# Rotary turn of the retention heads: DMA between partition halves in place of a product with a turning matrix

## The reference, cut to what matters

```python
def head_group_mixer(h, w_in, sb_norm, ret_norm, w_out):
    sb_q, sb_k, sb_v, r_q, r_k, r_v, r_g = jnp.split(h @ w_in, cuts, axis=-1)
    sb_o = stick_breaking(split_heads(sb_q, 8), split_heads(sb_k, 8), split_heads(sb_v, 8))
    ret_o = retention(rotary(split_heads(r_q, 4)), rotary(split_heads(r_k, 4)), split_heads(r_v, 4))
    ...
def rotary(x):          # x of 4 heads, 256 tokens, 128 features
    x1, x2 = xf[..., : d // 2], xf[..., d // 2:]
    return jnp.concatenate([x1 * cos - x2 * sin, x1 * sin + x2 * cos], axis=-1)
```

## Time and profile before

| | |
|---|---|
| median of three runs | 3829.74 us (3826.93 to 3830.98) |
| the profiled execution's own time | 3830.59 us |
| its span | 3828.8 us |
| PE busy | 3766.3 us, 98% |
| DVE busy | 2734.8 us, 71% |
| ACT busy | 1758.6 us, 46% |
| POOL busy | 572.9 us, 15% |
| mean granted TensorE clock | 0.994 |

### The profile page before, as it was taken

How to read it: one execution, slowest core, us unless ns; L and a number is a source line. 1 busy time by engine, 2 the same in 40 slices (tenths; PEclk the granted TensorE clock), 3 DMA queues, 4 the chain that set the end, 5 groups by cost and what they waited for, 6 DMA issues and landing times.

```text
span 3828.8 us, 68647 instructions
## 1 busy us (share of the span) xinstructions
PE 3766.3 (98%) x23022; PEld 3367.8 (88%) x23022; DVE 2734.8 (71%) x4796; ACT 1758.6 (46%) x2739; POOL 572.9 (15%) x244
## 2 busy tenths in 40 slices
PE   8999999999999999999999999999999999999999
PEld 6888888888888889998999999888889999998887
DVE  7867777676863556634578888888534598888887
ACT  3223323223322354456556776333464557774333
POOL 0000000000000000045575000000256680000000
PEclk9999999999999999999999999999999999999999
DMA  6544434454542325563456666777634466666776
GB/s 251 177 159 157 157 131 153 145 180 138 176 138 88 94 67 157 184 200 118 133 187 224 207 209 203 240 241 241 221 127 149 139 229 208 208 211 220 241 241 211
DMA packets 203862, 685.45 MB, mean 179 GB/s; under 512 B 22560, under 2 KB 24864, under 8 KB 194336
## 3 DMA queue, kind: packets, MB, share of 16 engines
q1 hardware_dynamic: 174880, 573.45, 46.4%
q10 hardware_dynamic: 28800, 109.59, 7.9%
HBM read 646.25 MB, written 36.70 MB: 178 GB/s over the span
## 4 chain that ended last, share of the span: by engine, by line
PE 81%; issue 9%; POOL 7%; DVE 2%; ACT 0%; POOLq 0%; DMA 0%; DVEq 0%; ACTq 0%; SPq 0%
PE bank L581 25%; PE bank L583 25%; PE bank L582 25%; POOL low L541 7%; PE bank L1117 2%; PE bank L623 1%; PE bank L676 0%; PE bank L677 0%; PE bank L681 0%; PE bank L784 0%; PE bank L762 0%; DVE h L1615 0%; DVE low L1636 0%; PE bank L651 0%; ACT high L1200 0%
## 5 line engine op out<-in xcount | busy, mean ns | idle before, releaser
L1200 ACT ACTIVATE high<-raw 128x1024 fp32r<-128x1024 f32 x1044 | 1098.8, 1057 | 1221.3 <-PE bank L583 941.5
L581 PE MATMUL bank<-h_lo,high 128*128 128x256 f32 (+1 forms) x4240 | 1321.8, 312 | 1.5 <-POOL low L541 0.9
L583 PE MATMUL bank<-h_hi,low 128*128 128x256 f32 (+1 forms) x4240 | 1318.4, 311 | 0.0
L582 PE MATMUL bank<-h_hi,high 128*128 128x256 f32 (+1 forms) x4240 | 1316.5, 310 | 0.0
L1636 DVE TENSOR_TENSOR low<-raw,high 128x1024 fp32r<-128x1024 f32 x808 | 971.6, 1219 | 82.1 <-ACT high L1200 79.8
L541 POOL TENSOR_TENSOR low<-raw,high 128x1024 fp32r<-128x1024 f32 x240 | 572.7, 2403 | 2584.5 <-ACT high L1200 2551.2
L581 PEld LDWEIGHTS bank<-h_lo,high 128*128 128x128 f32 x4240 | 799.3, 189 | 50.5 <-POOL low L541 1.8
L582 PEld LDWEIGHTS bank<-h_hi,high 128*128 128x128 f32 x4240 | 799.4, 189 | 47.0 <-issue 0.7
L583 PEld LDWEIGHTS bank<-h_hi,low 128*128 128x128 f32 x4240 | 798.7, 188 | 46.5
L581 PE MATMUL bank<-low,weighed_hi 128*128 128x512 f32 x1024 | 400.0, 391 | 8.5 <-DVE weighed_lo L1636 8.5
L583 PE MATMUL bank<-high,weighed_lo 128*128 128x512 f32 x1024 | 399.8, 390 | 0.0
(11 more groups left out here) (298 smaller groups left out, 4554.2 us busy)
## 6 DMA issues: line engine op xcount, KB each, us to landing
raw<-in_experts SPq DMA_DIRECT2D x516, 512.0 KB, 3.4
raw<-in_w SPq DMA_DIRECT2D x176, 512.0 KB, 4.2
late_raw<-in_mod_late ACTq DMA_DIRECT2D x64, 1024.0 KB, 4.8
acts_spill<-acts_out ACTq DMA_DIRECT2D x128, 256.0 KB, 4.0
acts_in<-acts_spill SPq DMA_DIRECT2D x128, 256.0 KB, 3.4
raw<-in_w_in SPq DMA_DIRECT2D x56, 512.0 KB, 3.4
raw<-in_w SPq DMA_DIRECT2D x64, 384.0 KB, 3.1
raw<-in_w SPq DMA_DIRECT2D x64, 320.0 KB, 3.6
```

The source lines that it names most:

```text
L581: pe.matmul(out, a[0], b[1], start=start, stop=False, **more)
L582: pe.matmul(out, a[0], b[0], start=False, stop=False, **more)
L583: return pe.matmul(out, a[1], b[0], start=False, stop=stop, **more)
L1200: act.activation(high[:, slot * UNIT:(slot + 1) * UNIT], raw[:, slot * UNIT:(slot + 1) * UNIT], ACT.Copy)\
```

## The change: what it does

The turning matrix goes, from the constants and from PE. In its place ACT issues DMAs that copy the halves of the partitions of `r_qk` crosswise into `turned`: partitions 64 to 127 to partitions 0 to 63 and the other way round, four tiles (256 KB) in each DMA. Two DMAs for tiles 0 to 3 are issued after the copy of tile 4, two for tiles 4 to 7 after `high_of` of the memory. Each pair has its own semaphore. The sign of the turn moves into the sine table, whose first 64 partitions are negated on the host.

On DVE the rotary work (two products and an addition for each pair of tiles) moves ahead of the wait for z and the maximum; the product with the sine is now made in place in `turned` and no longer reads a bank. The four additions that raise `head_ready` move with it, from behind the masks of the softplus. POOL's wait for `head_ready` and its place stay as they are, and so do ACT's clamp and exponential.

```diff
@@ PE
                 wait("split", KD)
                 T["normed"].next(KD)
-                for c in range(4):
-                    pe.matmul(ps[4 + c][:, :], mix_const("turn_ret"), r_qk[:, 2 * c:2 * c + 2, :], start=True, stop=True)\
-                        .then_inc(S["head_turned"], 1)
                 wait("z_copied", 4)
@@ ACT
-                to_sbuf([r_qk[:, c, :] for c in range(8)])
+                def swap_halves(first):
+
+                    act.wait_ge(S["evacuated"], T["evacuated"].value(first + 14))
+                    for to in (0, HD // 2):
+                        start = HD // 2 - to
+                        act.dma_start(turned[to:to + HD // 2, first * TOK:(first + 4) * TOK],
+                                      r_qk[start:start + HD // 2, first:first + 4, :].rearrange("p c t -> p (c t)"))\
+                            .then_inc(S[f"swapped{first}"], 16)
+
+                to_sbuf([r_qk[:, c, :] for c in range(5)])
+                swap_halves(0)
+                to_sbuf([r_qk[:, c, :] for c in range(5, 8)], first=5)
                 high_of(mem_hi, mem)
+                swap_halves(4)
                 rows_to_sbuf([r_v[:, s, :] for s in range(2)], 4, bank=4)
@@ DVE
+                wait("mix_loaded", 16)
+                for half in range(2):
+                    wait(f"swapped{4 * half}", 32)
+                    for c in (2 * half, 2 * half + 1):
+                        part, other = r_qk[:, 2 * c:2 * c + 2, :], turned[:, c * 512:(c + 1) * 512].rearrange("p (g t) -> p g t", g=2)
+                        for tile, table in ((other, sin_r), (part, cos_r)):
+                            mark(dve.tensor_tensor(tile, tile, table.rearrange("p (g t) -> p g t", g=1)
+                                                   .to_broadcast([P, 2, TOK]), ALU.mult))
+                        settle()
+                        dve.tensor_tensor(part, part, other, ALU.add).then_inc(S["head_ready"], 1)
+
                 wait("z_copied", SBH)
                 mark(dve.tensor_scalar(stick[:, :], z[:, :], 0.0, None, ALU.max))
-
-                wait("mix_loaded", 16)
-                for c in range(4):
-                    wait("head_turned")
-                    mark(dve.tensor_tensor(turned[:, c * 512:(c + 1) * 512].rearrange("p (g t) -> p g t", g=2),
-                                           ps[4 + c][:, :].rearrange("p (g t) -> p g t", g=2),
-                                           sin_r.rearrange("p (g t) -> p g t", g=1).to_broadcast([P, 2, TOK]), ALU.mult))
-                    mark(dve.tensor_tensor(r_qk[:, 2 * c:2 * c + 2, :], r_qk[:, 2 * c:2 * c + 2, :],
-                                           cos_r.rearrange("p (g t) -> p g t", g=1).to_broadcast([P, 2, TOK]), ALU.mult))
                 settle()
...
-                for c in range(4):
-                    dve.tensor_tensor(r_qk[:, 2 * c:2 * c + 2, :], r_qk[:, 2 * c:2 * c + 2, :],
-                                      turned[:, c * 512:(c + 1) * 512].rearrange("p (g t) -> p g t", g=2), ALU.add)\
-                        .then_inc(S["head_ready"], 1)
@@ constants
-            lay([one[n] for n in MIX_CONSTS] + [np.cos(ret), np.sin(ret), decay.reshape(P, -1)]))
+            lay([one[n] for n in MIX_CONSTS] + [np.cos(ret), np.where(i[:, None] < HD // 2, -1, 1) * np.sin(ret), decay.reshape(P, -1)]))
```

More of the change, by code:

```diff
@@ L74 @@
 CONST_COLS = P * len(CONSTS) + 1
-MIX_CONSTS = ["ones64", "tri", "causal", "turn_ret"]
+MIX_CONSTS = ["ones64", "tri", "causal"]
 MIX_COLS = P * len(MIX_CONSTS) + 2 * TOK + RH * SPAN
@@ L89 @@
     "stick_exp": SBH, "broken": 1, "broken_o": 1,
-    "head_turned": 4, "head_ready": 4, "ret_scored": RH, "ret_decayed": RH, "ret_o": 1,
+    "swapped0": 32, "swapped4": 32, "head_ready": 4, "ret_scored": RH, "ret_decayed": RH, "ret_o": 1,
     "head_summed": 3, "head_rooted": 2, "head_inverted": 2, "head_scaled": 2, "mean_ready": 1, "centred": 1, "mixed_ready": 1,
@@ L395, in two_blocks @@
             "head_summed", "head_rooted", "head_inverted", "head_scaled", "head_normed", "head_turned", "head_ready",
+            "swapped0", "swapped4",
             "score_ready", "max_ready", "exp_ready", "prob_ready", "flipped", "flip_copied", "pv_ready", "o_copied",
@@ L1276, in activate_tiles, with to_sbuf @@
                     tile(f, late + n // 4 * 4 + f if is_late else None)
-            def to_sbuf(outs, func=ACT.Copy):
-                for u, out in enumerate(outs):
+            def to_sbuf(outs, func=ACT.Copy, first=0):
+                for u, out in enumerate(outs, first):
                     wait("unit_used")
@@ L2262, in constant_columns @@
     }
[L2263 to L2270, removed]
+    turn = np.zeros((P, P))
+    for c in range(P):
+        if c // 32 % 2 == 0:
+            turn[c + 32, c] = -1
+        else:
+            turn[c - 32, c] = 1
+    one["turn_axial"] = turn
     f = np.float32
```

## The result

| | before | after |
|---|---|---|
| median | 3830.36 us (3826.93 to 3833.64, 6 runs) | 3845.80 us (3844.02 to 3848.12, 6 runs) |
| ratio to before | | 1.0041, 95% interval 1.0031 to 1.0051 |
| span of the profiled run | 3828.8 us | 3846.3 us |
| clock, mean | 0.994 | 0.991 |

The change makes the kernel 15.4 us slower: 3845.8 us, against a forecast of 3842. The two profiled runs differ by more, 17.5 us, because the one after (3848.12 us) is the slowest of its six. First the page of the kernel after: busy time, share of the span, instructions.

A forecast was written before the change was run, and what follows sets the result against it. The prediction took PE as the limit over the whole kernel. Two layers of 5.5 us delay plus 0.8 us clock loss gave 12.6 us on the profiled 3830.6, so 3843.2, or 3842 in medians; range 3824 to 3848.

The forecast's parts named there:

- The gate opens early, the masks take turns with POOL: Before the stick additions: four second-half masks alternate with POOL's parts, 10.7 us instead of 1.4; first stick addition 7.7 us later.
- The taking of turns without the clock: From projections to scores, the delay per layer before any clock loss: +5.5 us, bounds -3.1 to +8.
- The rotary work beside POOL: On DVE before z: rotary instructions alternate with POOL's parts, 2.95 us a turn, done at 1752.0; PE hardly pushed back.
- Turn products off PE: Before the memory keys: 3.13 us of PE products go; keys start 1.5 us earlier once other delays are counted.
- The DMA issues on ACT: Four issues a layer; the last two delay the high parts behind the memory's split by 0.5 us, bounds 0 to 0.8.
- a sign of being wrong: In the r_g units: PE waiting for POOL by more than 1 us each would show the prediction wrong.
- The transfers: 256 KB copies between halves of the on-chip memory: 4 us each, not late even at 10 us.
- The clock: Idle PE before the later stick sums lowers its clock: 0.8 us a layer, out of 0 to 1.7.
- clock falls for longer: Rival, behind PE's wait: clock loss of 1.7 us in full, perhaps twice, a layer; 3843 to 3848, taken as 3846; chance 0.12.
- The sum: Whole kernel, two layers: 2 x (5.5 + 0.8) = 12.6 us slower, 3842 in medians.
- Not slower: Rival: masks and POOL's four parts do not collide, 2.7 us a layer gained, 3824; decided by POOL starting after 1759; chance 0.22.
- DVE gets two instructions to one part: Rival: two DVE instructions pass per POOL part, so masks wait only twice; +2 us a layer, 3834; chance 0.12.

The follow-up runs named there:

- kernel with 24 fillers: The changed kernel with 24 small unused products on PE behind the sum of stick head 3, keeping PE busy in its wait: 3843.15 us, 1.0028.
- late gate: The changed kernel with POOL's gate before unit 32 waiting for all eight softplus masks instead of the rotary sums: 3830.21 us, 1.0002.
- mask in a bank: The changed kernel, its gate still early, with the causal mask copied into free bank 7 and read there by the masks: 3830.38 us, 0.9998.
- moving the issues: The changed kernel with POOL's gate behind the masks and the second pair of DMAs issued ahead of the memory's splits: 3829.65 us, 0.9991.
- the cleared line: The changed kernel, gate early, second DMA pair issued ahead of the memory's splits, mask and cosine and sine tables read from bank 7: 3826.19 us, 0.9989.

## Why the prediction was right, step by step

- **The gate opens early, the masks take turns with POOL.** Right, the large term: forecast 10.7 us for four masks, measured 9.96. POOL had already begun its first part when they came. The first stick addition came 6.3 us later in the stage, not 7.7, and behind it 1.7 us are won back at full clock, forecast 2.2 (the retention scores start 5.2 us after the first addition in the kernel with 24 fillers, forecast 4.9; from there to the product with the values it is 5.7, forecast 5.4). The taking of turns without the clock is so 4.7 us a layer, forecast 5.5. Both undoings (late gate, mask in a bank) give the whole loss back.
- **The rotary work beside POOL.** Right: 2.7 to 2.9 us for each instruction beside a part, done at 1751.1, forecast 1752.0; three and not two ran before POOL started. As forecast it did not delay the stage, since the softplus was what DVE waited for next (0.40 us at 1756.59).
- **Turn products off PE.** Right that only part of their 3.13 us comes back: keys 1.1 us earlier in the stage, forecast 1.5. The next thing late was the copies of z.
- **The DMA issues on ACT.** Too small. Two issues took 1.12 us and the first high part behind them started 1.06 us later in the stage (1726.65 against 1725.30), forecast 0.5 and bound 0.8. PE waited 1.65 us for POOL at the first `r_g` unit, 0.45 in the kernel before. That is over the 1 us that the prediction had named as a sign of being wrong if it came at each of these units; it came at the first alone. With the masks in the way it hardly counts; with the late gate, moving the issues takes 0.9 and 0.7 us off the two stages.
- **The transfers.** Right: none was waited for.
- **The clock.** Too small: forecast 0.8 a layer out of 0 to 1.7, measured 2.6 and 1.3, over the upper bound in the first layer. The step took the stretch around 1652 as its measure, where the half speed was 3.4 us long; in the first layer it lasted from about 1767.7 to 1774.5, 5.6 of its 6.8 us behind the wait, over sums that the next steps wait for. The rival "clock falls for longer", 3846, gave the closest time; it is the forecast's own mechanism with this term at full size.
- **The sum.** Forecast 2 x 6.3 = 12.6 us, measured in the two stages 13.2: the turns 1.7 us smaller in the two layers together, the clock 2.3 larger. That the sum comes so close is luck in part, two errors that nearly cancel; the mechanism doesn't rest on it. Of the other 4.3 us of span, 2.1 are only the difference between the profiled pair and the medians. By place, 0.3 lie before the first stage, 2.5 between the two and 1.5 behind the second, where the trace has longer stretches at half speed than before. For one between the layers, windows of the kernel before and of the kernel after over nearly the same work (both hold a wait of PE of 4.25 us for `weighed_lo`):

```profile
2370.00:2380.00 10.00, 5.75 (x38) 5.17 (x38) 8.04 (x14) 4.85 (x10) 0.00 (x0) 0.93 0.62 190
```

```profile
2380.00:2390.00 10.00, 5.75 (x33) 5.07 (x32) 7.36 (x13) 4.22 (x9) 0.00 (x0) 0.78 0.64 194
```

  Over the next 10 us the clock is 0.90 and 0.88, so the whole stretch at half speed is some 3.4 us before and 6.8 after. The two layers of the kernel after show the same spread, with 6.8 and 3.4 us at half speed about waits of 5.8 us in both. No run separates these stretches from the change; why they came out longer here stays open.
- **Rivals.** "Not slower" fell: it was said to decide when POOL starts after 1759, and POOL started at 1757.85. "DVE gets two instructions to one part" fell: in both stretches each part of POOL let one instruction through.

## What to carry to other kernels

Before a DVE instruction is moved, look at which semaphore it raises and what GpSimd does once that opens: here a wait that seemed idle time of GpSimd kept its subtractions away from masks that PE needed. Where an instruction of DVE must run beside GpSimd, put its constant operand (a mask, a table) into a free bank; that took 9.96 us to 1.42 and made the order indifferent. An instruction with a single tensor input there, like the maximum above, is held up all the same and gains nothing by it. And work taken off the busiest engine is worth what the next wait of that engine ends on: 3.1 us of products off PE brought nothing while DVE's line was the longer one. Once that was cleared the stage was 2.6 us shorter, of which 2.3 are there already when the memory keys start (29.2 us into the stage, against 31.4). That these are the turn products is argued: no run has the cleared line with the products still on PE.

## What the runs showed of the hardware

A DMA from one half of the partitions to the other, 64 partitions of 4 KB, held ACT's queue for 0.47 to 0.62 us, against 0.35 for the load in the earlier trace rows and 0.45 for the load of `tables_m` behind it. Half of them landed within 3.7 us, about as fast as the load of 256 KB in the earlier trace rows (3.4), the slowest in 6.9. The group of these issues in the kernel after (count, shortest, median and longest ns), and their time to landing:

```profile
L1402 ACTq DMA_DIRECT2D turned<-r_qk x8: 469/571/620, 1708.9 to 2820.9; - x8
...
DMA to landing us min/median/max: 3.1/3.7/6.9
```

Idle time of 5.8 us on PE cost 2.6 us more behind it through the clock in one layer and 1.3 in the other, by the kernel with 24 fillers. The prediction had half of 1.7 us there.
